# A third seven-product step in the gate and up projections of a two-layer decoder trunk

## The chip, the cores and the metric

The kernel runs on one core of a Trainium2 chip. The metric is the device time of one execution in microseconds (us); lower is better. All arithmetic is in float32: every weight matrix is split into a high part and a low part, and every product is made as three matmuls (high by high, high by low, low by high).

## The reference

```python
def swiglu(h, w_gate, w_up, w_down):
    return (jax.nn.silu(h @ w_gate) * (h @ w_up)) @ w_down

def reference(x, ...):
    for i in range(DEPTH):                      # DEPTH = 2
        h = rms_norm(x, norm_mix[i])
        mix = gla_mixer(h, ...) if i % 2 == 0 else fox_mixer(h, ...)
        x = x + mix
        h = rms_norm(x, norm_ffn[i])
        x = x + swiglu(h, ffn_w_gate[i], ffn_w_up[i], ffn_w_down[i])
    return x
```

The sequence has 256 rows, the model dimension is 2048 and the hidden dimension of the feed-forward part is 5632. The change touches `h @ w_gate` and `h @ w_up` alone.

## The kernel before

**Chunks.** Weights stream from memory in chunks of 256 x 512 floats (512 KB). SyncE loads a chunk into one of four slots of `raw`; ScalarE rounds it into `w_hi` (a copy, L791); VectorE subtracts to get `w_lo` (L1279); TensorE then uses it. Slots are reused in a ring of four: ScalarE may round chunk n only when TensorE has used chunk n-4 (semaphore `chunk_used`), TensorE may start chunk n when `lo_done` has counted it. Each engine runs its instructions in the order in which they are written.

**A gate/up tile.** The hidden dimension is cut in 11 tiles of 512 columns (FT = 11). A tile takes 16 chunks: eight of gate (t = 0) and eight of up (t = 1), chunk j holding rows 256 j to 256 j + 255 of the weight. TensorE gathers gate in `acc[:, 0]` and up in `acc[:, 1]`. A chunk taken plainly ("one") is four products of 128 x 128 by 128 x 512, so twelve matmuls. In tiles 1 to 9 of each layer some pairs of chunks (gate j and up j) are instead taken together in a "seven" step: a 2 x 2 block product (two row blocks of x against two column tiles) with seven products in place of eight, so 21 matmuls in place of 24. VectorE makes four differences of weight blocks for it (`g_raw`: L1429, L1432, L1435), ScalarE rounds them (`g_hi`, L870), VectorE makes their low parts (`g_lo`, L1444); of the second chunk of the pair only the lower half is split (L865, L1439). Four of the products go to banks of their own (`seven_acc`), and are added to gate and up at the end of the tile. The sums of x blocks that the seven products need (`xs_hi`, `xs_lo`) are made once per layer, during tile 0 (`x_sums`, L1398 to L1405, then L883 and L1412).

**Order.** `ORDER_GU` is the order of the 16 chunks of tiles 1 to 9, and all four engines walk it. Before, it is: gate 2 to 5; step 0; gate 6 and 7; step 1; up 2 to 7. The steps thus stand at positions 4, 5 and 8, 9 of the tile (positions count from 0).

**Work that hangs on positions.** On VectorE, at position 2 `hidden_joined` finishes the tile before: it adds `acc[:, 1]` to the sums (L1610) and multiplies by the activated gate (L1616, into `stage`, signal `staged`). At position 3 `squares_h` transposes `stage` (L1349), after which GpSimd issues sixteen small DMAs (L2028). At position 14 the first product is read out by ScalarE (L877) and added (L1452); at position 15 the other sums follow (L1457, L1459, L1461), gate is joined (L1464), and the transposed tile is split (L909, L1357). In tiles 1 and 2, `sums` (L1366 to L1369) follows there as well. Tile 1's position 2 has the plain `hidden` (L1584) for tile 0. `g_raw`, `g_lo` and the product sums `g_sum` lie in the same memory.

The ScalarE job `silu_joined` (L975) stands at position 1 and waits for `gate_joined`.

Of the kernel before, what the change touches and what calls it, by code (L numbers as in the profile page):

```python
# [30 lines left out]
F32 = mybir.dt.float32  # L31
F32R = mybir.dt.float32r
# [5 lines left out]
P = 128  # L38
# [38 lines left out]
def build(nc, x, norm_mix, norm_ffn, gla_w_in, gla_w_g2, gla_b_g2, gla_o_gain, gla_w_o,  # L77
# [38 lines left out]
    def down_order(steps, first, gaps):  # L116
# [3 lines left out]
        for j, gap in enumerate(gaps + (len(rest),)):  # L120
# [4 lines left out]
    ORDER = [[down_order(SEVEN, 6, (4, 4, 4))] * 2,  # L125
             [down_order(6, 8, (3, 3, 2, 2, 2)), down_order(8, 5, (2,) * 7)]]
    GU0, GU1 = 1, FT - 1
    PAIRS = 2
    GU = PAIRS * (GU1 - GU0)
    ORDER_GU = [("one", 0, j) for j in range(2, 6)] + [("seven", 0, 0), ("seven", 1, 0), ("one", 0, 6), ("one", 0, 7),  # L130
                                                       ("seven", 0, 1), ("seven", 1, 1)] \
        + [("one", 1, j) for j in range(2, CH)]

    def down_step(layer, pp, j):
        return layer * (GU + DT // 2 * SEVEN) + GU + pp * STEPS[layer][0] + j
# [21 lines left out]
    with ctx:  # L157
        def sb(name, shape, dt=F32):
            return ctx.enter_context(nc.sbuf_tensor(name, shape, dt))
# [33 lines left out]
        hscale = sb("head_scale", [P, TB * 4])  # L193
        gqk = sb("fox_gains", [P, 1])
        psc = sb("psc", [P, 3, TB * 4])
        narrow = sb("narrow", [R, S])
        diag = sb("diag", [P, TB, P])
        ohr = sb("o_rstd", [P, GH, TB])
# [75 lines left out]
        xs_hi, xs_lo = (at(f"x_sum_{i}", [P, PAIRS, 4, P], (32 + 44 * (i == "lo")) * K, F32R) for i in ("hi", "lo"))  # L274
        xs_raw = at("x_sum_raw", [P, PAIRS, 4, P], 76 * K)
# [125 lines left out]
        def _(pe):  # L401
# [82 lines left out]
            def gate_up(layer, c_up, i):  # L484

                c = gate_chunk(c_up, i)
                step = gate_step(layer, i)
                block0, block1 = slice(0, P), slice(P, S)
                upper, lower = slice(0, N), slice(N, 2 * N)
                for n, (kind, t, j) in enumerate(ORDER_GU):  # L490
                    a = (c.base + n) % SLOTS
                    if kind == "seven" and t == 0:
                        b, first, last = a + 1, j == 0, j == PAIRS - 1
                        k = KC_CHUNK * j
                        wait(pe, lo_done, c + (n + 2))
                        if isinstance(i, int) and first:
                            pe.wait_ge(x_sum_lo, layer + 1)
                        three(seven_acc[0], xt_hi[:, k, block0], xt_lo[:, k, block0], w_hi[:, a, upper],
                              w_lo[:, a, upper], first, last)
                        three(acc[:, 0, 0, :], xt_hi[:, k + 1, block0], xt_lo[:, k + 1, block0], w_hi[:, a, lower],  # L500
                              w_lo[:, a, lower], False, last).then_inc(chunk_used, 1)
                        three(acc[:, 1, 0, :], xs_hi[:, j, 3, :], xs_lo[:, j, 3, :], w_hi[:, b, lower],
                              w_lo[:, b, lower], first, False).then_inc(chunk_used, 1)
                        wait(pe, diff_lo, (step + (j + 1)) * 2 + (-1))
                        three(seven_acc[1], xs_hi[:, j, 0, :], xs_lo[:, j, 0, :], g_hi[:, 0, :], g_lo[:, 0, :], first, last)
                        three(seven_acc[3], xs_hi[:, j, 2, :], xs_lo[:, j, 2, :], g_hi[:, 1, :], g_lo[:, 1, :], first, last)
                        wait(pe, diff_lo, (step + (j + 1)) * 2)
                        three(seven_acc[2], xs_hi[:, j, 1, :], xs_lo[:, j, 1, :], g_hi[:, 2, :], g_lo[:, 2, :], first, last)
# [268 lines left out]
        def _(ac):  # L777
# [102 lines left out]
            def x_sums_hi(layer):  # L880

                ac.wait_ge(x_sum_raw, layer + 1)
                nc.scalar.activation(xs_hi[:, :, :, :], xs_raw[:, :, :, :], ACT.Copy).then_inc(x_sum_hi, 1)  # L883

            def squares(n, norm, t):

# [380 lines left out]
        def _(ve):  # L1267
# [126 lines left out]

            def x_sums(layer):

                both = slice(0, PAIRS * KC_CHUNK)
                link(nc.vector.tensor_tensor(hraw[:, both, :], xt_hi[:, both, :].bitcast(F32),  # L1398
                                             xt_lo[:, both, :].bitcast(F32), ALU.add))
                src = hraw[:, both, :].rearrange("p (j r) (b t) -> p j r b t", r=KC_CHUNK, t=P)  # L1400
                a11, a12, a21, a22 = (src[:, :, r, b, :] for b in range(TB) for r in range(KC_CHUNK))
                nc.vector.tensor_tensor(xs_raw[:, :, 2, :], a11, a21, ALU.subtract)
                link(nc.vector.tensor_tensor(xs_raw[:, :, 0, :], a21, a22, ALU.add))
                link(nc.vector.tensor_tensor(xs_raw[:, :, 1, :], xs_raw[:, :, 0, :], a11, ALU.subtract))
                nc.vector.tensor_tensor(xs_raw[:, :, 3, :], a12, xs_raw[:, :, 1, :],  # L1405
                                        ALU.subtract).then_inc(x_sum_raw, 1)

            def x_sums_low(layer):

                ve.wait_ge(x_sum_raw, layer + 1)  # L1410
                ve.wait_ge(x_sum_hi, layer + 1)
                nc.vector.tensor_tensor(xs_lo[:, :, :, :], xs_raw[:, :, :, :], xs_hi[:, :, :, :].bitcast(F32),  # L1412
                                        ALU.subtract).then_inc(x_sum_lo, 1)

            def gate_up(layer, c_up, i, hidden, turn, swap):
# [4 lines left out]
                for n, (kind, t, j) in enumerate(ORDER_GU):  # L1420
# [16 lines left out]
                    if (kind, t) == ("seven", 1):  # L1437
# [3 lines left out]
                        for half in range(2):  # L1441
# [1 line left out]
                            wait(ve, diff_hi, (step + (j + 1)) * 2 + (half - 1))  # L1443
                            nc.vector.tensor_tensor(g_lo[:, pair, :], g_raw[:, pair, :], g_hi[:, pair, :].bitcast(F32),  # L1444
                                                    ALU.subtract).then_inc(diff_lo, 1)
                    if n == 2:
                        hidden()
                    if n == 3:
                        swap()
                    if n == 14:  # L1450
                        wait(ve, p1_gate, gate_count(layer, i) + 1)
# [2 lines left out]
                    if n == 15:  # L1454
                        wait(ve, moved, gate_tile(layer, i) * 256)
                        wait(ve, gate_sums, sums + 1)
                        nc.vector.tensor_tensor(g_sum[:, 1, :], seven_acc[3], g_sum[:, 2, :],  # L1457
                                                ALU.add).then_inc(gate_sums, 1)
                        nc.vector.tensor_tensor(g_sum[:, 2, :], seven_acc[1], g_sum[:, 2, :], ALU.add)  # L1459
                        wait(ve, gate_sums, sums + 2)  # L1460
                        nc.vector.tensor_tensor(g_sum[:, 3, :], seven_acc[1], g_sum[:, 1, :],  # L1461
                                                ALU.add).then_inc(gate_sums, 1)
                        wait(ve, chunk_used, c + 10)
                        nc.vector.tensor_tensor(act[:, :, :], acc[:, 0, :, :], g_sum[:, 0:2, :],  # L1464
                                                ALU.add).then_inc(gate_joined, 1)
                    if n == 15:
# [93 lines left out]
            def out_and_ffn(c_o, g_o, c_up, g_up, c_down, g_down, m, norm, first, first_turn, saved):  # L1560
# [44 lines left out]
                def hidden_joined(i):  # L1605
# [1 line left out]
                    end = gate_chunk(c_up, i)  # L1607
                    wait(ve, chunk_used, end)
                    wait(ve, gate_sums, gate_count(layer, i, 3))
                    nc.vector.tensor_tensor(g_sum[:, 2:4, :], acc[:, 1, :, :], g_sum[:, 2:4, :],  # L1610
                                            ALU.add).then_inc(up_joined, 1)
                    wait(ve, gate_done, (Lin(i) if isinstance(i, int) else Lin(0, 1, i)) + layer * FT)
                    wait(ve, turned, (Lin(i) if isinstance(i, int) else Lin(0, 1, i)) + (g_up - 1))
                    wait(ve, up_joined, gate_count(layer, i))
                    for b in range(TB):
                        last = nc.vector.scalar_tensor_tensor(  # L1616
                            out=stage[:, b, :], in0=g_sum[:, 2 + b, :], scalar=rstd[:, norm, b:b + 1],
                            in1=act[:, b, :], op0=ALU.mult, op1=ALU.mult)
                    last.then_inc(staged, 1)

# [546 lines left out]
```

## Time and profile before

| | |
|---|---|
| median of 3 runs | 2277.46 us (2277.4 to 2277.67) |
| the profiled execution: its time, its span | 2278.0 us, 2275.7 us |
| TensorE matmul busy | 2267.3 us (100% of the span), 10242 matmuls |
| VectorE busy | 1737.7 us (76%) |
| ScalarE busy | 1211.2 us (53%) |
| GpSimd busy | 341.9 us (15%) |
| share of the 16 DMA engines, weights' queue | 61.9% |

The span is the time from the first to the last instruction of the profiled execution; the 2.3 us between it and the time of that execution lie outside of what the engines do. Busy matmul time counts the union of overlapping matmuls: a matmul is shown as 389 ns long, while the next one starts much sooner.

### The profile page before, as it was taken

How to read it: one execution, taken by the hardware profiler on the slowest of the kernel's cores; microseconds unless marked ns; L12 is line 12 of the kernel's file. 1: busy time of each engine (PE TensorE's matmuls, PEld its weight loads, DVE VectorE, ACT ScalarE, POOL GpSimd, SP SyncE). 2: the span in 40 equal slices, each digit the busy share in tenths (PEclk: the TensorE clock that was granted, in tenths of full speed). 3: DMA queues.
4: the chain of work that ended last, by engine and by line, in shares of the span. 5: the costliest groups of instructions: out<-in, count | busy, mean ns of one | idle time of the engine just before them, and what ended most of it. 6: DMA issues, size and time to landing. Idle time of an engine off the chain costs nothing.

```text
span 2275.7 us, 28590 instructions
## 1 busy us (share of the span) xinstructions
PE 2267.3 (100%) x10242; PEld 1878.1 (83%) x10242; DVE 1737.7 (76%) x2049; ACT 1211.2 (53%) x1563; POOL 341.9 (15%) x558
## 2 busy tenths in 40 slices
PE   9999999999999999999999999999999999999999
PEld 7888878888888888888888888888888888888887
DVE  6888558688888877887577855568788888868787
ACT  5545554555555554454566656445555555545454
POOL 2036210111211211000223200001112112111000
PEclk9999999999999999999999999999999999999999
DMA  7655545666666666565758876655666666666664
GB/s 220 185 176 158 174 158 185 199 215 215 199 225 204 209 220 214 189 202 195 193 170 208 213 181 166 155 174 191 219 196 221 214 202 212 221 203 205 218 205 158
DMA packets 241211, 447.53 MB, mean 197 GB/s; under 512 B 23236, under 2 KB 25384, under 8 KB 241112
## 3 DMA queue, kind: packets, MB, share of 16 engines
q1 hardware_dynamic: 224416, 430.49, 61.9%
q0 software_dynamic: 12304, 15.24, 2.0%
q10 hardware_dynamic: 4392, 0.50, 0.2%
q8 instruction: 58, 0.95, 0.2%
q14 instruction: 41, 0.34, 0.0%
HBM read 432.52 MB, written 2.11 MB: 191 GB/s over the span
## 4 chain that ended last, share of the span: by engine, by line
PE 98%; DVE 1%; ACT 1%; DMA 0%; issue 0%; ACTq 0%; SPq 0%
PE acc L451 16%; PE acc L452 16%; PE acc L453 16%; PE acc L442 14%; PE acc L444 14%; PE acc L443 14%; PE wk L453 1%; PE wk L452 1%; PE tp L453 1%; PE tp L452 1%; PE wk L451 1%; PE tp L451 1%; PE wk L671 1%; DVE w_lo L1279 0%; PE tp L409 0%; PE wk L728 0%
## 5 line engine op out<-in xcount | busy, mean ns | idle before, releaser
L1279 DVE TENSOR_TENSOR w_lo<-raw,w_hi 128x1024 fp32r<-128x1024 f32 x758 | 933.0, 1249 | 394.7 <-ACT w_hi L791 389.9
L791 ACT ACTIVATE w_hi<-raw 128x1024 fp32r<-128x1024 f32 x758 | 796.7, 1060 | 701.5 <-PE acc L453 339.7
L442 PE MATMUL acc<-w_hi,xt_hi 128*128 128x512 f32 x1152 | 454.7, 395 | 2.2 <-DVE w_lo L1279 2.1
L444 PE MATMUL acc<-w_hi,xt_lo 128*128 128x512 f32 x1152 | 448.8, 390 | 0.0
L443 PE MATMUL acc<-w_lo,xt_hi 128*128 128x512 f32 x1152 | 448.4, 389 | 0.0
L451 PE MATMUL acc<-w_hi,xt_hi 128*128 128x512 f32 x900 | 350.1, 389 | 0.0
L452 PE MATMUL acc<-w_lo,xt_hi 128*128 128x512 f32 x900 | 350.1, 389 | 0.0
L453 PE MATMUL acc<-w_hi,xt_lo 128*128 128x512 f32 x900 | 350.1, 389 | 0.0
L2028 POOL DMA_DIRECT2D ht_raw<-act x352 | 173.0, 499 | 775.8 <-DVE act L1349 746.0
L442 PEld LDWEIGHTS acc<-w_hi,xt_hi 128*128 128x128 f32 x1152 | 216.3, 188 | 50.7 <-issue 3.3
L444 PEld LDWEIGHTS acc<-w_hi,xt_lo 128*128 128x128 f32 x1152 | 216.2, 188 | 45.5
L443 PEld LDWEIGHTS acc<-w_lo,xt_hi 128*128 128x128 f32 x1152 | 216.4, 188 | 44.7 <-issue 1.0
L451 PE MATMUL acc<-w_hi,ht_hi 128*128 128x512 f32 x550 | 213.9, 389 | 0.0
L452 PE MATMUL acc<-w_lo,ht_hi 128*128 128x512 f32 x550 | 213.9, 389 | 0.0
L453 PE MATMUL acc<-w_hi,ht_lo 128*128 128x512 f32 x550 | 213.9, 389 | 0.0
L453 PEld LDWEIGHTS acc<-w_hi,xt_lo 128*128 128x128 f32 x900 | 168.9, 188 | 35.3
L452 PEld LDWEIGHTS acc<-w_lo,xt_hi 128*128 128x128 f32 x900 | 168.9, 188 | 35.1
L451 PEld LDWEIGHTS acc<-w_hi,xt_hi 128*128 128x128 f32 x900 | 168.9, 188 | 34.9
L451 PEld LDWEIGHTS acc<-w_hi,ht_hi 128*128 128x128 f32 x550 | 103.2, 188 | 21.6
L452 PEld LDWEIGHTS acc<-w_lo,ht_hi 128*128 128x128 f32 x550 | 103.2, 188 | 21.4
L453 PEld LDWEIGHTS acc<-w_hi,ht_lo 128*128 128x128 f32 x550 | 103.2, 188 | 21.3
L870 ACT ACTIVATE gate_diff_hi<-gate_diff_raw 128x1024 fp32r<-128x1024 f32 x72 | 76.6, 1063 | 59.4 <-DVE gate_diff_raw L1429 45.1
(322 smaller groups left out, 2666.8 us busy)
## 6 DMA issues: line engine op xcount, KB each, us to landing
raw<-in_ffn_w_gate_dram SPq DMA_DIRECT2D x176, 512.0 KB, 3.9
raw<-in_ffn_w_up_dram SPq DMA_DIRECT2D x176, 512.0 KB, 4.6
raw<-in_ffn_w_down_dram SPq DMA_DIRECT2D x176, 512.0 KB, 4.4
raw<-in_fox_w_in_dram SPq DMA_DIRECT2D x128, 512.0 KB, 5.5
raw<-in_gla_w_in_dram SPq DMA_DIRECT2D x96, 512.0 KB, 4.5
raw<-in_gla_w_o_dram SPq DMA_DIRECT2D x32, 512.0 KB, 4.2
raw<-in_fox_w_o_dram SPq DMA_DIRECT2D x32, 512.0 KB, 4.0
ht_raw<-act POOLq DMA_DIRECT2D x352, 32.0 KB, 3.3
```

What stands on the lines that cost most here:

```text
L442: pe.matmul(o, xh, wh, start=(k == 0), stop=False)
L443: pe.matmul(o, xh, wl, start=False, stop=False)
L444: last = pe.matmul(o, xl, wh, start=False, stop=(k == chunks * KC_CHUNK - 1))
L451: pe.matmul(o, xh, wh, start=start, stop=False)
L452: pe.matmul(o, xh, wl, start=False, stop=False)
L453: return pe.matmul(o, xl, wh, start=False, stop=stop)
L671: last = pe.matmul(wk[:, b, h * P:(h + 1) * P], ks, qs, start=(kf == 0), stop=(kf == FPH - 1))
L791: nc.scalar.activation(w_hi[:, slot, :], raw[:, slot, :], ACT.Copy).then_inc(hi_done, 1)
L870: nc.scalar.activation(g_hi[:, two, :], g_raw[:, two, :], ACT.Copy).then_inc(diff_hi, 1)
L1279: nc.vector.tensor_tensor(w_lo[:, slot, :], raw[:, slot, :], w_hi[:, slot, :].bitcast(F32), ALU.subtract).then_inc(lo_done, 1)
L2028: po.dma_start(hraw[Q * j:Q * j + Q, i, :], ht_sq[Q * i:Q * i + Q, j, :]).then_inc(moved, 16)
```

## The change

`PAIRS` goes from 2 to 3, so each of tiles 1 to 9 takes three pairs of chunks in seven-product steps. The new order is: gate 3; step 0; gate 4 and 5; step 1; gate 6 and 7; step 2; up 3 to 7. The steps stand at positions 1, 2, then 5, 6, then 9, 10. `hidden_joined` moves from position 2 to 3 and `squares_h` from 3 to 4. TensorE gets a new wait on `staged` in the first step, ahead of the product that overwrites `acc[:, 1, 0]`; VectorE waits for `gate_joined` before the first differences. Two of the product sums go to `stage` instead of `g_sum`, and the gated product is made in place there. The sums of x for the third pair get memory of their own.

```diff
-    PAIRS = 2
+    PAIRS = 3
-    ORDER_GU = [("one", 0, j) for j in range(2, 6)] + [("seven", 0, 0), ("seven", 1, 0), ("one", 0, 6), ("one", 0, 7),
-                                                       ("seven", 0, 1), ("seven", 1, 1)] \
-        + [("one", 1, j) for j in range(2, CH)]
+    ORDER_GU = [("one", 0, 3)]
+    for j in range(PAIRS):
+        ORDER_GU += [("seven", 0, j), ("seven", 1, j)] + [("one", 0, 4 + 2 * j + m) for m in range(2) if j + 1 < PAIRS]
+    ORDER_GU += [("one", 1, j) for j in range(PAIRS, CH)]
@@ sums of x for the third pair
+        xs2_hi = at("x_sum2_hi", [P, 1, 4, P], 92 * K, F32R)
+        xs2_lo, xs2_raw = over("x_sum2_lo", [P, 1, 4, P], x_sum_at, F32R), over("x_sum2_raw", [P, 1, 4, P], x_sum_at)
@@ TensorE, gate_up, in a seven step
                         three(acc[:, 0, 0, :], xt_hi[:, k + 1, block0], xt_lo[:, k + 1, block0], w_hi[:, a, lower],
                               w_lo[:, a, lower], False, last).then_inc(chunk_used, 1)
-                        three(acc[:, 1, 0, :], xs_hi[:, j, 3, :], xs_lo[:, j, 3, :], w_hi[:, b, lower],
+                        if first:
+                            wait(pe, staged, Lin(G[f"ffn{layer}"] + i) if isinstance(i, int) else Lin(G[f"ffn{layer}"], 1, i))
+                        three(acc[:, 1, 0, :], sum_h[:, 3, :], sum_l[:, 3, :], w_hi[:, b, lower],
                               w_lo[:, b, lower], first, False).then_inc(chunk_used, 1)
@@ ScalarE, x_sums_hi
-                nc.scalar.activation(xs_hi[:, :, :, :], xs_raw[:, :, :, :], ACT.Copy).then_inc(x_sum_hi, 1)
+                nc.scalar.activation(xs_hi[:, :, :, :], xs_raw[:, :, :, :], ACT.Copy)
+                nc.scalar.activation(xs2_hi[:, :, :, :], xs2_raw[:, :, :, :], ACT.Copy).then_inc(x_sum_hi, 1)
@@ VectorE, x_sums
-                both = slice(0, PAIRS * KC_CHUNK)
-                link(nc.vector.tensor_tensor(hraw[:, both, :], xt_hi[:, both, :].bitcast(F32),
-                                             xt_lo[:, both, :].bitcast(F32), ALU.add))
+                link(nc.vector.tensor_tensor(hraw[:, :, :], xt_hi[:, 0:4, :].bitcast(F32), xt_lo[:, 0:4, :].bitcast(F32),
+                                             ALU.add))
+                link(x_pairs(hraw[:, :, :], xs_raw))
+                rest = slice(4, PAIRS * KC_CHUNK)
+                link(nc.vector.tensor_tensor(hraw[:, 0:KC_CHUNK, :], xt_hi[:, rest, :].bitcast(F32),
+                                             xt_lo[:, rest, :].bitcast(F32), ALU.add))
+                x_pairs(hraw[:, 0:KC_CHUNK, :], xs2_raw).then_inc(x_sum_raw, 1)
+
+            def x_pairs(x, dst):
+
+                src = x.rearrange("p (j r) (b t) -> p j r b t", r=KC_CHUNK, t=P)
                 a11, a12, a21, a22 = (src[:, :, r, b, :] for b in range(TB) for r in range(KC_CHUNK))
+                nc.vector.tensor_tensor(dst[:, :, 2, :], a11, a21, ALU.subtract)
+                link(nc.vector.tensor_tensor(dst[:, :, 0, :], a21, a22, ALU.add))
+                link(nc.vector.tensor_tensor(dst[:, :, 1, :], dst[:, :, 0, :], a11, ALU.subtract))
+                return nc.vector.tensor_tensor(dst[:, :, 3, :], a12, dst[:, :, 1, :], ALU.subtract)
@@ VectorE, x_sums_low: a second subtraction of 128 x 512 for xs2_lo
@@ VectorE, gate_up
                         wait(ve, diff_used, step + j)
+                        if j == 0:
+                            wait(ve, gate_joined, gate_count(layer, i))
...
-                    if n == 2:
+                    if n == 3:
                         hidden()
-                    if n == 3:
+                    if n == 4:
                         swap()
...
-                        nc.vector.tensor_tensor(g_sum[:, 2, :], seven_acc[1], g_sum[:, 2, :], ALU.add)
+                        wait(ve, turned, gate_tile(0, i) + G[f"ffn{layer}"])
+                        nc.vector.tensor_tensor(stage[:, 0, :], seven_acc[1], g_sum[:, 2, :], ALU.add)
                         wait(ve, gate_sums, sums + 2)
-                        nc.vector.tensor_tensor(g_sum[:, 3, :], seven_acc[1], g_sum[:, 1, :],
+                        nc.vector.tensor_tensor(stage[:, 1, :], seven_acc[1], g_sum[:, 1, :],
                                                 ALU.add).then_inc(gate_sums, 1)
-                        wait(ve, chunk_used, c + 10)
+                        wait(ve, chunk_used, c + 11)
@@ VectorE, hidden_joined
-                    nc.vector.tensor_tensor(g_sum[:, 2:4, :], acc[:, 1, :, :], g_sum[:, 2:4, :],
+                    nc.vector.tensor_tensor(stage[:, :, :], acc[:, 1, :, :], stage[:, :, :],
                                             ALU.add).then_inc(up_joined, 1)
...
-                            out=stage[:, b, :], in0=g_sum[:, 2 + b, :], scalar=rstd[:, norm, b:b + 1],
+                            out=stage[:, b, :], in0=stage[:, b, :], scalar=rstd[:, norm, b:b + 1],
```

## Rows read from the trace of the kernel before

**Rows 1.** The page: busy time of the engines, and the granted clock in 40 slices.

```profile
PE 2267.3 (100%) x10242; PEld 1878.1 (83%) x10242; DVE 1737.7 (76%) x2049; ACT 1211.2 (53%) x1563; POOL 341.9 (15%) x558
...
PEclk9999999999999999999999999999999999999999
```

**Rows 2.** The page: the chain that ended last, by engine.

```profile
PE 98%; DVE 1%; ACT 1%; DMA 0%; issue 0%; ACTq 0%; SPq 0%
```

**Rows 3.** Busy time by stretch: one whole gate/up tile of layer 0.

```profile
603.50:645.70 42.20, 42.20 (x188) 34.95 (x187) 35.75 (x38) 22.87 (x25) 7.84 (x16) 1.00 0.67 211
```

**Rows 4.** Timeline of PE: start, length, engine, line, names, count; 614.71 starts a tile.

```profile
600.65 0.39 PE L452 MATMUL acc<-w_lo,xt_hi 128*128 128x512 f32 x1
...
614.71 0.39 PE L451 MATMUL acc<-w_hi,xt_hi 128*128 128x512 f32 x1
...
622.41 0.39 PE L452 MATMUL acc<-w_lo,xt_hi 128*128 128x512 f32 x1
```

**Rows 5.** Timeline of DVE around the same start of a tile; idle before in brackets.

```profile
605.12 1.23 DVE L1279 TENSOR_TENSOR w_lo<-raw,w_hi 128x1024 fp32r<-128x1024 f32 x1 [0.89 <-ACT w_hi L791]
...
610.32 2.35 DVE L1279 TENSOR_TENSOR w_lo<-raw,w_hi 128x1024 fp32r<-128x1024 f32 x2
...
615.00 1.23 DVE L1610 TENSOR_TENSOR gate_product_sums<-acc,gate_product_sums 128x1024 f32<-128x1024 f32 x1 [0.50 <-PE acc L453]
616.26 1.42 DVE L1616 SCALAR_TENSOR_TENSOR stage<-gate_product_sums,rstd,act 128x512 f32<-128x512 f32 x2
617.60 1.22 DVE L1279 TENSOR_TENSOR w_lo<-raw,w_hi 128x1024 fp32r<-128x1024 f32 x1
618.73 1.30 DVE L1349 STREAM_TRANSPOSE act<-stage 128x512 f32<-128x512 f32 x2
...
621.05 1.22 DVE L1429 TENSOR_TENSOR gate_diff_raw<-raw 128x1024 f32<-128x1024 f32 x1
...
623.64 0.69 DVE L1439 TENSOR_TENSOR w_lo<-raw,w_hi 128x512 fp32r<-128x512 f32 x1
...
626.51 2.36 DVE L1279 TENSOR_TENSOR w_lo<-raw,w_hi 128x1024 fp32r<-128x1024 f32 x2
```

**Rows 6.** Timeline of ACT in the same tile: second half of a step, next rounding.

```profile
623.76 1.06 ACT L870 ACTIVATE gate_diff_hi<-gate_diff_raw 128x1024 fp32r<-128x1024 f32 x1 [0.39 <-DVE gate_diff_raw L1435]
...
628.42 1.06 ACT L791 ACTIVATE w_hi<-raw 128x1024 fp32r<-128x1024 f32 x1 [1.57 <-DMA raw<-in_ffn_w_gate_dram]
```

**Rows 7.** Timeline of DVE at the end of tile 1, layer 0: `sums`.

```profile
483.90 0.42 DVE L1366 TENSOR_TENSOR sum_raw<-ht_raw 128x256 f32<-128x256 f32 x1
...
485.49 3.49 DVE L1279 TENSOR_TENSOR w_lo<-raw,w_hi 128x1024 fp32r<-128x1024 f32 x3
```

**Rows 8.** Timelines of DVE, ACT, PE, end of tile 0 (layer 0); 446.07 starts tile 1.

```profile
434.96 1.22 DVE L1398 TENSOR_TENSOR ht_raw<-xt_hi,xt_lo 128x1024 f32<-128x1024 f32 x1
...
437.47 0.42 DVE L1405 TENSOR_TENSOR x_sum_raw<-ht_raw,x_sum_raw 128x256 f32<-128x256 f32 x1
...
441.11 1.22 DVE L1412 TENSOR_TENSOR x_sum_lo<-x_sum_raw,x_sum_hi 128x1024 fp32r<-128x1024 f32 x1
...
446.27 1.41 DVE L1584 SCALAR_TENSOR_TENSOR stage<-acc,rstd,act 128x512 f32<-128x512 f32 x2 [0.34 <-PE acc L444]
...
438.89 3.06 ACT L791 ACTIVATE w_hi<-raw 128x1024 fp32r<-128x1024 f32 x3
...
446.07 0.39 PE L451 MATMUL acc<-w_hi,xt_hi 128*128 128x512 f32 x1
```

**Rows 9.** Timelines of DVE and PE: a wait of TensorE near the start of the kernel.

```profile
21.63 1.23 DVE L1279 TENSOR_TENSOR w_lo<-raw,w_hi 128x1024 fp32r<-128x1024 f32 x1
...
23.00 0.47 PE L442 MATMUL acc<-w_hi,xt_hi 128*128 128x512 f32 x1 [0.70 <-DVE w_lo L1279]
23.31 0.40 PE L443 MATMUL acc<-w_lo,xt_hi 128*128 128x512 f32 x1
```

**Rows 10.** Groups by line and shape: a subtraction or sum of 128 x 128 on DVE.

```profile
L1924 DVE TENSOR_TENSOR fox_p<-fox_p,masks 128x128 f32<-128x128 f32 x16 | 4.7, 292 | 0.5
```

More of the change, by code:

```diff
@@ L127, in build @@
     GU0, GU1 = 1, FT - 1
-    PAIRS = 2
+    PAIRS = 3
     GU = PAIRS * (GU1 - GU0)
-    ORDER_GU = [("one", 0, j) for j in range(2, 6)] + [("seven", 0, 0), ("seven", 1, 0), ("one", 0, 6), ("one", 0, 7),
-                                                       ("seven", 0, 1), ("seven", 1, 1)] \
-        + [("one", 1, j) for j in range(2, CH)]
+    ORDER_GU = [("one", 0, 3)]
+    for j in range(PAIRS):
+        ORDER_GU += [("seven", 0, j), ("seven", 1, j)] + [("one", 0, 4 + 2 * j + m) for m in range(2) if j + 1 < PAIRS]
+    ORDER_GU += [("one", 1, j) for j in range(PAIRS, CH)]
+    assert len(ORDER_GU) == 2 * CH
     def down_step(layer, pp, j):
@@ L195, in build @@
         psc = sb("psc", [P, 3, TB * 4])
+        x_sum_at = nc.sbuf_base
         narrow = sb("narrow", [R, S])
@@ L273, in build @@
         g_raw, g_sum = at("gate_diff_raw", [P, 4, N], 80 * K), at("gate_product_sums", [P, 4, N], 80 * K)
-        xs_hi, xs_lo = (at(f"x_sum_{i}", [P, PAIRS, 4, P], (32 + 44 * (i == "lo")) * K, F32R) for i in ("hi", "lo"))
-        xs_raw = at("x_sum_raw", [P, PAIRS, 4, P], 76 * K)
+        xs_hi, xs_lo = (at(f"x_sum_{i}", [P, 2, 4, P], (32 + 44 * (i == "lo")) * K, F32R) for i in ("hi", "lo"))
+        xs_raw = at("x_sum_raw", [P, 2, 4, P], 76 * K)
+        xs2_hi = at("x_sum2_hi", [P, 1, 4, P], 92 * K, F32R)
+        assert base + room[0] <= nc.sbuf_usable_end
+        xs2_lo, xs2_raw = over("x_sum2_lo", [P, 1, 4, P], x_sum_at, F32R), over("x_sum2_raw", [P, 1, 4, P], x_sum_at)
+        XS = [(xs_hi[:, 0], xs_lo[:, 0]), (xs_hi[:, 1], xs_lo[:, 1]), (xs2_hi[:, 0], xs2_lo[:, 0])]
         d_hi = over("diff_hi", [P, 4, N], xt_at + xt_half, F32R)
@@ L493, in gate_up @@
                         b, first, last = a + 1, j == 0, j == PAIRS - 1
+                        sum_h, sum_l = XS[j]
                         k = KC_CHUNK * j
@@ L501, in gate_up @@
                               w_lo[:, a, lower], False, last).then_inc(chunk_used, 1)
-                        three(acc[:, 1, 0, :], xs_hi[:, j, 3, :], xs_lo[:, j, 3, :], w_hi[:, b, lower],
+                        if first:
+                            wait(pe, staged, Lin(G[f"ffn{layer}"] + i) if isinstance(i, int) else Lin(G[f"ffn{layer}"], 1, i))
+                        three(acc[:, 1, 0, :], sum_h[:, 3, :], sum_l[:, 3, :], w_hi[:, b, lower],
                               w_lo[:, b, lower], first, False).then_inc(chunk_used, 1)
                         wait(pe, diff_lo, (step + (j + 1)) * 2 + (-1))
-                        three(seven_acc[1], xs_hi[:, j, 0, :], xs_lo[:, j, 0, :], g_hi[:, 0, :], g_lo[:, 0, :], first, last)
-                        three(seven_acc[3], xs_hi[:, j, 2, :], xs_lo[:, j, 2, :], g_hi[:, 1, :], g_lo[:, 1, :], first, last)
+                        three(seven_acc[1], sum_h[:, 0, :], sum_l[:, 0, :], g_hi[:, 0, :], g_lo[:, 0, :], first, last)
+                        three(seven_acc[3], sum_h[:, 2, :], sum_l[:, 2, :], g_hi[:, 1, :], g_lo[:, 1, :], first, last)
                         wait(pe, diff_lo, (step + (j + 1)) * 2)
-                        three(seven_acc[2], xs_hi[:, j, 1, :], xs_lo[:, j, 1, :], g_hi[:, 2, :], g_lo[:, 2, :], first, last)
+                        three(seven_acc[2], sum_h[:, 1, :], sum_l[:, 1, :], g_hi[:, 2, :], g_lo[:, 2, :], first, last)
                         three(acc[:, 0, 1, :], xt_hi[:, k + 1, block1], xt_lo[:, k + 1, block1], g_hi[:, 3, :],
@@ L1395, in x_sums @@
             def x_sums(layer):
-                both = slice(0, PAIRS * KC_CHUNK)
-                link(nc.vector.tensor_tensor(hraw[:, both, :], xt_hi[:, both, :].bitcast(F32),
-                                             xt_lo[:, both, :].bitcast(F32), ALU.add))
-                src = hraw[:, both, :].rearrange("p (j r) (b t) -> p j r b t", r=KC_CHUNK, t=P)
-                a11, a12, a21, a22 = (src[:, :, r, b, :] for b in range(TB) for r in range(KC_CHUNK))
[L1402 to L1406, printed above, removed]
+                link(nc.vector.tensor_tensor(hraw[:, :, :], xt_hi[:, 0:4, :].bitcast(F32), xt_lo[:, 0:4, :].bitcast(F32),
[7 more added lines that the diff above has]
+                src = x.rearrange("p (j r) (b t) -> p j r b t", r=KC_CHUNK, t=P)
+                a11, a12, a21, a22 = (src[:, :, r, b, :] for b in range(TB) for r in range(KC_CHUNK))
+                nc.vector.tensor_tensor(dst[:, :, 2, :], a11, a21, ALU.subtract)
+                link(nc.vector.tensor_tensor(dst[:, :, 0, :], a21, a22, ALU.add))
+                link(nc.vector.tensor_tensor(dst[:, :, 1, :], dst[:, :, 0, :], a11, ALU.subtract))
+                return nc.vector.tensor_tensor(dst[:, :, 3, :], a12, dst[:, :, 1, :], ALU.subtract)
             def x_sums_low(layer):
@@ L1411, in x_sums_low @@
                 ve.wait_ge(x_sum_hi, layer + 1)
-                nc.vector.tensor_tensor(xs_lo[:, :, :, :], xs_raw[:, :, :, :], xs_hi[:, :, :, :].bitcast(F32),
+                nc.vector.tensor_tensor(xs_lo[:, :, :, :], xs_raw[:, :, :, :], xs_hi[:, :, :, :].bitcast(F32), ALU.subtract)
+                nc.vector.tensor_tensor(xs2_lo[:, :, :, :], xs2_raw[:, :, :, :], xs2_hi[:, :, :, :].bitcast(F32),
                                         ALU.subtract).then_inc(x_sum_lo, 1)
```

## The prediction, as put on record before the result was known

> **What bounds the kernel now.** The page comes first: TensorE's matmuls cover the whole span and the granted clock is in its top tenth in every slice, the 2.4 GHz level [rows 1]. The chain that ended last is 98% TensorE [rows 2]. So time is the number of matmuls times their spacing, plus every wait of TensorE. The spacing is read from start to start, not from the 0.39 us that a matmul is shown to last: the first and the last of these rows are 96 matmuls apart, 21.76 us, so 0.2267 us each [rows 4]. A gate/up tile of 186 matmuls then takes 42.16 us, and the stretch of one tile agrees, with TensorE busy throughout [rows 3]. TensorE has no slack to give, and each matmul less is worth 0.2267 us as long as nobody makes it wait.
>
> Who could? In that tile VectorE is busy 35.75 of 42.2 us, ScalarE 22.87 [rows 3]. VectorE is the next one, so the question is how much work it gets and, more, where. VectorE's idle time there stands before splits of weight chunks, waiting for ScalarE, which waits for TensorE to free one of four slots [rows 5]. The 6.4 us of slack can thus not be saved up: VectorE runs at most three chunks ahead.
>
> **What is removed.** Each third step makes 21 matmuls of 24. That is 3 x 9 tiles x 2 layers = 54 matmuls, 54 x 0.2267 = 12.2 us, all on the path: a gain if nothing else happens.
>
> **What is added to VectorE and ScalarE.** A step, from the first difference to the next plain split, takes VectorE 626.51 - 621.05 = 5.46 us, where the one plain split it replaces takes 618.73 - 617.60 = 1.13 [rows 5]. So 4.33 us more per tile: 35.8 + 4.3 = 40.1 of a tile that would be 183 x 0.2267 = 41.5 us long. It fits as a sum, with 1.4 us to spare. ScalarE gets two roundings of 1.06 us [rows 6] and saves about half of one, some 1.7 us on 22.9, which hides.
>
> **Where it falls.** I count from the first matmul of a tile, 614.71 before [rows 4]. The last split of the tile before starts at 605.12, so at -9.59, held back by a slot and not by VectorE's own backlog (0.89 idle) [rows 5]. That hold stays, because the tile's last five chunks stay plain. Between it and the first split of the new tile (610.32, at -4.39) VectorE works without a gap on the product sums, the joined gate and the turned tile [rows 5]. The same instructions stand there after the change; that two of them write to `stage` I cost at nothing, since size and source stay (bounds: 0 to 0.1 us a tile).
>
> From there the order is new. Splits 0 and 1: 2 x 1.13, to -2.13. Step 0: 5.46, to 3.33. Split 3: 1.13, to 4.46. Only now comes `hidden_joined`, whose two parts take from 615.00 to 616.26 + 1.42, or 2.68 us [rows 5]: `staged` at 7.14. ScalarE keeps up: its last rounding for a step starts at 623.76, 2.71 after the step's first difference [rows 6], so it ends at -2.13 + 2.71 + 1.06 = 1.64, and the rounding of chunk 3, about 1 us, is done by 2.7.
>
> TensorE takes chunk 0 (12 matmuls) and the first six of step 0, and then stands at its new wait on `staged`, at 18 x 0.2267 = 4.08. What is queued behind it are the other 15 matmuls of the step and the whole rest of the tile; ScalarE's roundings wait for those through the slots. From the end of a VectorE split to TensorE's first matmul after a real wait it takes 23.00 - (21.63 + 1.23) = 0.14 us, and the second matmul comes 0.31 after the first in place of 0.23, 0.08 more [rows 9]. So TensorE resumes at 7.28: **a wait of 3.20, with the restart 3.28 us, in each ordinary tile**, against 0.68 us saved there. The rest of step 0 is not late: the half split it needs ends at -2.13 + (623.64 - 621.05) + 0.69 = 1.15 [rows 5], asked at 2.72; the low differences end by about 3.4, asked at 4.76 and 6.12. Even with nothing else to do VectorE could not sign before 0.3 + 2.68, the old place [rows 5].
>
> Steps 1 and 2 I cost at nothing. Their cover is the two plain chunks between steps, 5.4 us, as long as VectorE's 5.46 of a step starts at once when TensorE leaves the step before. The low parts of differences are then ready some 2 us before they are asked. Without this cover a late step would cost its lateness. The third load pair is requested when the half split of the step before is done and lands some 4 us later (ScalarE waits for such a load until 628.42, 4.1 us after that split's end at 624.33) [rows 5, 6]; in the new order that is 6 us or more before TensorE needs the split, so DMA stays hidden. Bounds: 0 to 1 us a tile.
>
> **Tiles 2 and 3** come after the tiles in which VectorE also makes `sums`: 485.49 - 483.90 = 1.59 us more between joined gate and first split [rows 7]. That hides today and no longer will: 3.28 + 1.59 = 4.87 us each.
>
> **Tile 1** has the longer `x_sums` ahead of it [rows 8]. Today they end at 437.47 + 0.42 = 437.89 and ScalarE rounds the last chunk of tile 0 from 438.89. The third pair adds a sum of 128 x 512 (0.69 us as the split of that size [rows 5]) and four of 128 x 128 (0.29 each [rows 10]), about 1.95 us in all, and to ScalarE about 0.55. So that rounding starts at 441.4, its split ends at 443.7, and TensorE, asking at 446.07 - 2.72 = 443.35, waits 0.5. The low parts (1.13 + 0.6) come next, then splits 0 and 1: TensorE waits another 0.2 for the first and starts the tile at 446.74; step 0 starts at 447.65. Its half split ends at 450.93, with 0.14 at 451.07, asked at 449.46: 1.6. `staged` comes at 447.65 + 5.46 + 1.13 + 1.41 (the plain form, L1584 [rows 8]) = 455.65, with 0.14 at 455.79, asked at 452.43: 3.35. Four waits and restarts: 0.5 + 0.2 + 1.6 + 3.35 + 0.3 = 5.95. Bounds 4.5 to 7.
>
> **The sum.** A layer: 5.95 + 2 x 4.87 + 6 x 3.28 = 35.4; two layers 70.7. Less 12.2: +58.5. Against the profiled execution's own 2278.0 us that is 2336.5; the median of the runs lies 0.5 us lower, so **2336**. The terms' bounds (steady wait 3.0 to 3.6, tile 1, restart) give 2329 to 2344 for this case by itself.
>
> **Rivals.**
>
> *TensorE's clock falls.* The new waits are of 3.3 to 4.9 us, one a tile. The gaps that the trace shows are near the start and short (0.70 us in the row), and the clock holds [rows 1, 9]; so no row shows what a long one does. Half the clock for as long again as the wait would lose half of that time: for the four longest waits 4 x 4.9 / 2 = 10 us, 2346; for all eighteen (66 us of waits on `staged`) 33 us, 2369. Against it: each gap is followed by 41 us of dense matmuls, and most are only just over 3 us. Chance 14%. The Trainium skill, page "TensorE: Matmul & The Clock Gate", section "HAM oscillation — how this bites in real kernels", states this mechanism: waits that are long enough bring the array back to half its clock, over and over in one kernel. By that rule some of the longer waits here would be followed by matmuls at 1.2 GHz; no run here shows it.
>
> *Steps 1 or 2 become late too.* VectorE has 1.4 us to spare in a tile, and loads are asked for in pairs. If a load lands 1 to 2 us later than [rows 6] show, step 2 starts late. At 1 us a tile, 18 us more: 2354. For it speaks the tight sum, against it the 3.3 us by which the wait itself lengthens the tile, which is room for VectorE. Chance 8%.
>
> *No wait, only the gain.* This ends on the other side. VectorE would have to sign `staged` by 3.94 after the start of the tile, 3.2 earlier than I work out; it decides in its favour if step 0's work is mostly done before the tile starts. VectorE does have 6.4 us idle in a tile [rows 3], so a different gating of the last splits could allow it. Then 2278.0 - 12.2 = 2265.8, some 2265. With waits of just 0.68 us a tile, nothing would change. Against it: the splits 15, 0 and 1 and the differences stand in one queue, and 605.12 is set by TensorE's progress [rows 5]. Chance 4% for this, 3% for about no change.
>
> *Shorter waits.* If part of the queue is faster than read (step 0 overlapping more), 1 to 2 us a tile: 2290 to 2320. Chance 6%.
>
> **How the numbers follow.** The forecast has 65%, the rivals 14, 8, 4, 3 and 6. About 0.2% is what a measurement of this kernel can tell from no change, 4.6 us. Slower by more than that: 65 + 14 + 8 + 6, less a little, is 92%; within 3%, faster 5%. The range reaches from the upper part of shorter waits over the case itself (2329 to 2344) to late steps and a clock that falls a few times: 2320 to 2357.
>
> **What would show it.** In the profile after: 10188 matmuls; TensorE's waits led by one on VectorE's L1616-form (`stage`), some 16 times at 3.3 us and for four of them near 4.9, plus two for the plain form in tile 1; VectorE going from the joined gate to the in-place product without a gap; a tile of 44.8 us against 42.2. The prediction is wrong if that wait is missing or under 2 us, if TensorE's other waits sum to more than 10 us, or if the granted clock leaves its top level in the gate/up stretches.

## The result, and the profile after

The changed kernel takes 2373.51 us (median of 4 runs, 2367.37 to 2374.78) against 2277.57 us (median of 4): 4.15% slower, ratio 1.0415 with a 95% interval of 1.0403 to 1.0428. The forecast was 2336 us with a range of 2320 to 2357. The direction and the place were right; the size was 61% of what came, and the time lies outside the range.

The page after: busy time, the granted clock, the chain (they answer to [rows 1, 2]).

```profile
PE 2301.6 (97%) x10188; PEld 1893.6 (80%) x10188; DVE 1818.3 (77%) x2151; ACT 1242.9 (52%) x1601; POOL 342.2 (14%) x558
...
PEclk9999999999999999999999999999999998999999
...
PE 84%; DVE 10%; issue 3%; ACT 1%; DVEq 0%; DMA 0%; ACTq 0%; SPq 0%
```

There are 54 matmuls less, and yet TensorE is busy 34.3 us longer: the matmuls themselves must have become slower. The clock digits hide it, except for one slice with an 8, because a tenth is coarse. The list of TensorE's waits names who kept it:

```profile
PE acc L458 <- DVE stage L1637: 54.1, 16, 4.4
PE acc L458 <- DVE stage L1605: 6.1, 2, 3.1
PE tp L458 <- DVE w_lo L1459: 2.6, 2, 1.3
PE acc L449 <- DVE w_lo L1290: 2.1, 5, 1.0
```

That is the list the prediction asked for: 16 waits on the in-place product, 2 on the plain form in tile 1, 2 on the half split of tile 1. Only the last line's 2.1 us were there before. VectorE around the start of a tile after (the tile begins at 637.16, 18 matmuls before the wait; it answers to [rows 5]):

```profile
627.58 1.23 DVE L1290 TENSOR_TENSOR w_lo<-raw,w_hi 128x1024 fp32r<-128x1024 f32 x1 [2.49 <-ACT w_hi L801]
...
632.77 2.35 DVE L1290 TENSOR_TENSOR w_lo<-raw,w_hi 128x1024 fp32r<-128x1024 f32 x2
635.05 1.22 DVE L1449 TENSOR_TENSOR gate_diff_raw<-raw 128x1024 f32<-128x1024 f32 x1
...
638.24 2.35 DVE L1464 TENSOR_TENSOR gate_diff_lo<-gate_diff_raw,gate_diff_hi 128x1024 fp32r<-128x1024 f32 x2
640.51 1.22 DVE L1290 TENSOR_TENSOR w_lo<-raw,w_hi 128x1024 fp32r<-128x1024 f32 x1
641.64 1.22 DVE L1631 TENSOR_TENSOR stage<-acc,stage 128x1024 f32<-128x1024 f32 x1
642.97 1.41 DVE L1637 SCALAR_TENSOR_TENSOR stage<-stage,rstd,act 128x512 f32<-128x512 f32 x2
```

No bracket after the first row: from the last split of the old tile to the signature VectorE never stands still. And TensorE in the same tile (it answers to [rows 4]; the last matmul before the wait, then those after it):

```profile
641.01 0.39 PE L460 MATMUL acc<-w_hi,xt_lo 128*128 128x512 f32 x1
644.43 0.79 PE L458 MATMUL acc<-w_hi,x_sum_hi 128*128 128x512 f32 x1 [3.03 <-DVE stage L1637]
645.03 0.63 PE L459 MATMUL acc<-w_lo,x_sum_hi 128*128 128x512 f32 x1
645.45 0.63 PE L460 MATMUL acc<-w_hi,x_sum_lo 128*128 128x512 f32 x1
...
649.72 0.63 PE L458 MATMUL acc<-gate_diff_hi,xt_hi 128*128 128x512 f32 x1
650.15 0.46 PE L459 MATMUL acc<-gate_diff_lo,xt_hi 128*128 128x512 f32 x1
650.44 0.39 PE L460 MATMUL acc<-gate_diff_hi,xt_lo 128*128 128x512 f32 x1
650.67 0.40 PE L458 MATMUL acc<-w_hi,xt_hi 128*128 128x512 f32 x1
```

The wait is 644.43 - 641.01 - 0.23 = 3.19 us, where 3.20 was forecast. But the next matmuls stand 0.43 us apart, not 0.23, until 650.15. The windows say why (us, then busy time of PE, PEld, DVE, ACT, POOL, then the granted clock, DMA share, GB/s):

```profile
641.24:644.43 3.19, 0.16 (x1) 0.00 (x0) 3.09 (x5) 1.06 (x1) 0.00 (x0) 0.85 0.92 299
644.43:650.28 5.85, 5.84 (x14) 4.59 (x15) 3.41 (x4) 0.63 (x1) 3.24 (x7) 0.50 0.48 143
650.28:688.80 38.52, 38.52 (x171) 31.66 (x169) 33.36 (x35) 22.85 (x24) 4.61 (x10) 1.00 0.59 184
```

The clock fell to 0.50, 1.2 GHz, near the end of the wait and stayed there for 14 matmuls; then it was back at 2.4 GHz for the rest of the tile. It does not always fall within the wait. One tile earlier it was full throughout the same wait and fell about 1.1 us after TensorE had resumed:

```profile
594.76:597.96 3.20, 0.17 (x2) 0.01 (x1) 3.10 (x5) 1.06 (x1) 0.00 (x0) 1.00 0.94 312
597.96:602.50 4.54, 4.54 (x13) 3.62 (x14) 3.40 (x4) 0.63 (x1) 1.96 (x5) 0.62 0.52 155
```

The records of the granted clock show a low stretch, of 3.4 or 6.8 us, in or just behind each of the 18 waits on `staged`, at the longer and the shorter ones alike, 88.7 us in all; the kernel before has none but a last one as the program ends.

### The profile page after: what moved, and what is told of

It reads as the page before. It is cut to its first block, busy times and chain, and to the rows that moved or that the text cites. A ratio compares the mean times of both kernels' runs of the same rounds, so it can differ in the third digit from the quotient of the medians.

```text
span 2373.1 us, 28767 instructions
## 1 busy us (share of the span) xinstructions
PE 2301.6 (97%) x10188; PEld 1893.6 (80%) x10188; DVE 1818.3 (77%) x2151; ACT 1242.9 (52%) x1601; POOL 342.2 (14%) x558
## 4 chain that ended last, share of the span: by engine, by line
PE 84%; DVE 10%; issue 3%; ACT 1%; DVEq 0%; DMA 0%; ACTq 0%; SPq 0%
PE acc L449 13%; PE acc L451 13%; PE acc L450 13%; PE acc L458 11%; PE acc L459 11%; PE acc L460 11%; DVE w_lo L1290 3%; PE wk L458 2%; PE wk L459 2%; PE wk L460 2%; PE tp L460 1%; PE tp L459 1%; PE tp L458 1%; ACT w_hi L801 1%; DVE gate_diff_lo L1464 1%
## 5 line engine op out<-in xcount | busy, mean ns | idle before, releaser
L1290 DVE TENSOR_TENSOR w_lo<-raw,w_hi 128x1024 fp32r<-128x1024 f32 x740 | 911.1, 1249 | 360.1 <-ACT w_hi L801 355.9
L801 ACT ACTIVATE w_hi<-raw 128x1024 fp32r<-128x1024 f32 x740 | 777.4, 1060 | 613.6 <-PE acc L460 261.4
L449 PE MATMUL acc<-w_hi,xt_hi 128*128 128x512 f32 x1152 | 455.0, 395 | 2.4 <-DVE w_lo L1290 2.1
L451 PE MATMUL acc<-w_hi,xt_lo 128*128 128x512 f32 x1152 | 448.7, 390 | 0.0
L450 PE MATMUL acc<-w_lo,xt_hi 128*128 128x512 f32 x1152 | 448.5, 389 | 0.0
L458 PE MATMUL acc<-w_hi,xt_hi 128*128 128x512 f32 x774 | 301.4, 389 | 0.0
L459 PE MATMUL acc<-w_lo,xt_hi 128*128 128x512 f32 x774 | 301.2, 389 | 0.0
L460 PE MATMUL acc<-w_hi,xt_lo 128*128 128x512 f32 x774 | 301.1, 389 | 0.0
L449 PEld LDWEIGHTS acc<-w_hi,xt_hi 128*128 128x128 f32 x1152 | 216.3, 188 | 51.5 <-DVE w_lo L1290 4.3
L451 PEld LDWEIGHTS acc<-w_hi,xt_lo 128*128 128x128 f32 x1152 | 216.3, 188 | 45.8
L450 PEld LDWEIGHTS acc<-w_lo,xt_hi 128*128 128x128 f32 x1152 | 216.4, 188 | 44.3 <-issue 1.0
L880 ACT ACTIVATE gate_diff_hi<-gate_diff_raw 128x1024 fp32r<-128x1024 f32 x108 | 114.9, 1063 | 174.5 <-DVE gate_diff_raw L1449 153.5
L458 PEld LDWEIGHTS acc<-w_hi,xt_hi 128*128 128x128 f32 x774 | 145.4, 188 | 31.1 <-DVE w_lo L1290 0.5
L460 PEld LDWEIGHTS acc<-w_hi,xt_lo 128*128 128x128 f32 x774 | 145.3, 188 | 30.3
L459 PEld LDWEIGHTS acc<-w_lo,xt_hi 128*128 128x128 f32 x774 | 145.3, 188 | 30.2
L1464 DVE TENSOR_TENSOR gate_diff_lo<-gate_diff_raw,gate_diff_hi 128x1024 fp32r<-128x1024 f32 x108 | 127.1, 1219 | 0.0
```

What stands on the lines that cost most here:

```text
L449: pe.matmul(o, xh, wh, start=(k == 0), stop=False)
L450: pe.matmul(o, xh, wl, start=False, stop=False)
L451: last = pe.matmul(o, xl, wh, start=False, stop=(k == chunks * KC_CHUNK - 1))
L458: pe.matmul(o, xh, wh, start=start, stop=False)
L459: pe.matmul(o, xh, wl, start=False, stop=False)
L460: return pe.matmul(o, xl, wh, start=False, stop=stop)
```

## The experiments

Theory A: the waits cost what was forecast, and the rest, about 37 us, is the array at 1.2 GHz after each. Rival B: the rest is steps 1 and 2, late because VectorE is nearly full or loads land late.

**Filling the wait.** TensorE gets extra matmuls in front of the wait, whose result nobody reads.

```diff
                         if first:
+                            for _ in range(14):
+                                pe.matmul(seven_acc[3], xt_hi[:, k, block0], w_hi[:, b, lower], start=True, stop=True)
                             wait(pe, staged, ...)
```

> The changed kernel, with 14 extra matmuls of 512 columns into a bank that the step writes anew afterwards, put just ahead of TensorE's wait on `staged` in each of the 18 tiles; they take the place of most of the wait and add no result. Theory A (the waits are as long as forecast, and the rest of the loss is the array at 1.2 GHz after each of them): the wait of about 3.2 us shrinks to about 0.1 us in ordinary tiles and about 1.7 in tiles 2 and 3, the granted clock stays at its top level, and the time is 2332 to 2340 us, some 37 less than the changed kernel, though TensorE gets 252 matmuls more to do. Rival B (the rest of the loss is steps 1 and 2, late because VectorE is nearly full, or loads that land late): filling the wait changes nothing of that, 2368 to 2376 us.

2337.04 us, one run, granted clock 1.000. So with 252 matmuls more it is 36.5 us faster. Its list of waits:

```profile
PE acc L458 <- DVE stage L1639: 5.0, 4, 1.3
PE tp L458 <- DVE w_lo L1461: 2.6, 2, 1.3
```

In the twelve ordinary tiles no wait is listed any more, but its time is still spent, now on the extra matmuls (an ordinary tile takes 44.86 us, forecast 44.8). Nothing of what B names was touched, and B expected 2368 us or more: B is out. The price of the clock is 36.5 us, the distance to the changed kernel's median; against its single runs it is 30.3 to 37.7 us. Half as many matmuls:

> As the one with 14 extra matmuls, with 7 of them: the rest of the wait is about 1.6 us in ordinary tiles and 3.2 in tiles 2 and 3. Theory A: the clock falls in fewer tiles or in none but the four long ones, 2334 to 2350 us. If a rest of 1.6 us is enough to bring the clock down in every tile, the time stays near 2365 to 2372. Rival B: 2368 to 2376 whatever the filling.

2342.36 us, one run, clock 0.998.

```profile
PE acc L458 <- DVE stage L1639: 28.7, 16, 2.8
PE acc L458 <- DVE stage L1607: 3.0, 2, 1.5
```

After the fourteen rests of about 1.4 us (twelve of the first line, two of the second) the clock holds; of the four of about 2.8 us it falls in three (the records of the granted clock, 10.2 us low in all). One of these (start of tile 2, layer 0):

```profile
502.80 0.79 PE L458 MATMUL acc<-w_hi,x_sum_hi 128*128 128x512 f32 x1 [2.85 <-DVE stage L1639]
503.39 0.63 PE L459 MATMUL acc<-w_lo,x_sum_hi 128*128 128x512 f32 x1
```

Three falls for some 5 us more: about 1.7 us each.

**The early place without the third step.** Two steps as before, sums of x for two pairs, step 0 at positions 1 and 2.

```diff
-    PAIRS = 3
+    PAIRS = 2
+    ORDER_GU = [("one", 0, 2), ("seven", 0, 0), ("seven", 1, 0), ("one", 0, 3), ..., ("one", 0, 7),
+                ("seven", 0, 1), ("seven", 1, 1)] + [("one", 1, j) for j in range(PAIRS, CH)]
```

> The changed kernel without the third step: two steps as before, the first at positions 1 and 2 (the early place), the second at positions 8 and 9, sums of x for two pairs. It has the 10242 matmuls of the kernel before and VectorE's load of before. Theory A (the early place of step 0 costs, not the number of steps): waits on `staged` of 3.2 us in ordinary tiles and 4.8 in tiles 2 and 3 remain, with the clock falling after each, 2374 to 2390 us, slower than the changed kernel. Rival B (the third step's work fills VectorE, and that costs): 2278 to 2300 us.

2365.72 us, one run, 88 us slower than before with the same 10242 matmuls and VectorE's old load. Its waits:

```profile
PE acc L456 <- DVE stage L1629: 54.1, 16, 4.4
PE acc L456 <- DVE stage L1597: 4.5, 2, 2.3
```

The 54.1 us are those of the changed kernel to the tenth. So the place of the first step makes the wait, not the number of steps. The forecast of 2374 to 2390 was 8 us or more too high, again through the clock: with tiles of another length it fell at 14 of the 18 waits and was low for 51.2 us in the two layers' tiles, not for 88.7; over the first layer's tiles it was 0.97 of full where the changed kernel has 0.95. Equal waits do not bring equal falls.

**The product that waits, moved last.** The product that overwrites the up accumulator goes, with its wait, behind the other six.

```diff
-                        if first:
-                            wait(pe, staged, ...)
-                        three(acc[:, 1, 0, :], sum_h[:, 3, :], ...).then_inc(chunk_used, 1)
                         ...
                         three(acc[:, 0, 1, :], ...).then_inc(diff_used, 1)
+                        if first:
+                            wait(pe, staged, ...)
+                        three(acc[:, 1, 0, :], sum_h[:, 3, :], ...).then_inc(chunk_used, 1)
```

> The changed kernel, with the one product that overwrites the up accumulator, and the wait on `staged` ahead of it, moved behind the other six products of step 0 (of every step, in fact). It is asked for at 30 matmuls after the start of the tile, 6.80 us, instead of 18, 4.08 us, and `staged` still comes at about 7.3. Theory A: waits of 0.5 us in ordinary tiles, about 2.1 in tiles 2 and 3, about 3 in tile 1, in sum 22 us; the clock holds; less 12.2 us of removed matmuls that is 2284 to 2292 us. Rival B: 37 us remain on top of that, 2320 to 2328.

2299.17 us, ratio to before 1.0093 (1.0077 to 1.0110), clock 1.000: 74 us less than the changed kernel for one reordering. It is still 7 us above the forecast's top. A tile has two short waits where one was forecast:

```profile
629.85 0.50 PE L458 MATMUL acc<-w_hi,x_sum_hi 128*128 128x512 f32 x1 [0.31 <-DVE stage L1637]
...
636.50 0.50 PE L458 MATMUL tp<-w_hi,xt_hi 128*128 128x512 f32 x1 [0.21 <-DVE w_lo L1459]
```

The second is the half split of step 1, which VectorE now reaches too late: the long wait had given it room. And each costs more than it shows. An ordinary tile takes 42.75 us, 1.27 above 41.48, for 0.52 us of idle shown: about 0.37 us more per wait. Of this, 0.16 comes from the counting, since idle starts at a matmul's shown end, 0.16 after the next could start, and 0.11 from the restart, since the second matmul comes 0.34 after the first in place of 0.23. The rest was not traced.

**The join moved forward.** On VectorE, `hidden_joined` goes between the half split and the low parts of step 0.

```diff
                     if (kind, t) == ("seven", 1):
                         ... half split of the weights ...
+                        if j == 0:
+                            hidden()
                         for half in range(2):
                             ... low parts ...
-                    if n == 3:
-                        hidden()
```

> The changed kernel, with VectorE's joining of the tile before (`hidden_joined`, 2.68 us) moved from position 3 into step 0, between the half split and the low parts of the differences. Then `staged` comes at about 3.9 us after the start of the tile, asked for at 4.08: no wait there. The low differences come about 2.7 us later than in the changed kernel, 0.3 us after they are asked, and step 1's half split comes 0.3 to 0.6 late, as in the kernel with the product moved last. The clock holds. 0.3 + 0.4 us and two restarts of 0.2 to 0.4 a tile, 1.5 more in tiles 2 and 3, 3 in tile 1: 2288 to 2302 us. Rival: the wait on `staged` is due to something else in VectorE's queue, then 2320 or more.

2297.64 us, ratio 1.0088 (1.0073 to 1.0104), inside the range. The wait on `stage` is left in tiles 2 and 3 alone, 4.0 us in all; 10.7 us wait on half splits, 20 times: step 1 is late in the ordinary tiles.

**Everything spread.** On top of that, the transposing goes to position 6, the split of the turned tile to 13, the sums of x forward.

```diff
-                    if n == 4:
+                    if n == 6:
                         swap()
@@ ScalarE: turn() at 13 in place of 14; VectorE:
-                    if n == 15:
+                    if n == 13:
                         turn()
@@ tile 0, up half
-                tile(Lin(c_up), CH, mid=lambda: x_sums(norm // 2), ...)
+                tile(Lin(c_up), CH, late=lambda: x_sums(norm // 2), ...)
```

> As the one with the join first, and three more things moved to where VectorE sits idle: the transposing of the joined tile from position 4 to 6, behind step 1; the splitting of the turned tile (with `sums` in tiles 1 and 2) from position 15 (ScalarE: 14) to 13; the sums of x from position 6 to 3 in the second half of tile 0. All three steps and the 10188 matmuls stay. By the bookkeeping of VectorE's queue nothing is late in ordinary tiles, and some 0.6 us in tiles 2 and 3 at most: 2264 to 2270 us, faster than both kernels by the 12 us of the removed matmuls less a little. Rival (VectorE is too full for a third step wherever the pieces stand, 40.1 of 41.5 us a tile): waits of 0.5 us or more a tile remain, 2275 us or more.

2289.10 us, ratio 1.0053 (1.0039 to 1.0067): 19 us above its range. The time is one that the rival allowed (2275 us or more), but the trace gives another reason than a full VectorE. From start to start, nine of the eighteen tiles take 41.5 to 41.7 us, the other nine 42.0 to 44.9. GpSimd in a tile of 41.5 us that starts at 657.69, then ScalarE and VectorE in the same tile, and TensorE in the next one, which starts at 699.23 and takes 44.9:

```profile
673.56 1.96 POOL L2050 DMA_DIRECT2D ht_raw<-act  x4 [33.46 <-DVE act L1361]
679.48 5.87 POOL L2050 DMA_DIRECT2D ht_raw<-act  x12 [3.96 <-issue]
...
689.63 1.06 ACT L921 ACTIVATE ht_hi<-ht_raw 128x1024 f32 x1 [4.66 <-DMA ht_raw<-act]
690.59 1.04 ACT L801 ACTIVATE w_hi<-raw 128x1024 fp32r<-128x1024 f32 x1
...
690.93 1.23 DVE L1369 TENSOR_TENSOR ht_lo<-ht_raw,ht_hi 128x1024 f32 x1 [4.70 <-ACT ht_hi L921]
...
703.46 0.50 PE L458 MATMUL tp<-w_hi,xt_hi 128*128 128x512 f32 x1 [1.31 <-DVE w_lo L1460]
706.11 0.50 PE L458 MATMUL acc<-w_hi,x_sum_hi 128*128 128x512 f32 x1 [0.99 <-DVE stage L1638]
```

GpSimd stands still for 4 us between its fourth and fifth DMA. The moved tile lands 16 us after the transposing, ScalarE waits for it at position 13, and the roundings queued behind it are late; VectorE waits for them, and so comes late to the next tile. The same holds for all three such pauses in each layer's tiles 1 to 9: the six tiles behind them take 43.7 to 44.9 us, some 18 us too many in sum. The pauses are in the kernel before as well (2.0 to 4.5 us in the same three tiles of layer 0), where the tile has time to land.

**Spread, with room for the landing.** Two kernels, both with the transposing between step 1's half split and its low parts, and ScalarE's `turn()` at 14. In the first VectorE splits the turned tile at position 14, behind the first sum; in the second at 15, behind the joined gate.

```diff
                         if j == 0:
                             hidden()
+                        if j == 1:
+                            swap()
...
                     if n == 14:
                         wait(ve, p1_gate, ...)
                         ... L1473, the first sum ...
+                        turn()
```

> The spread kernel before it lost some 4 us in every second tile: GpSimd paused for 4 us between two of its sixteen small DMAs, the moved tile landed some 16 us after the transposing, and ScalarE, in order, stood before the split of the turned tile at position 13 and held the last roundings. Here the transposing stands within step 1, between its half split and its low parts (2.3 us earlier), and the split of the turned tile at position 14, on ScalarE behind the read-out of the first product, on VectorE behind the first sum. Theory: the landing at about 30 us of the tile no longer holds anything, ordinary tiles take 41.5 to 41.8 us in both kinds, tiles 2 and 3 about 2 us more: 2268 to 2276 us, faster than before. Rival: the low parts of step 1, now 1.2 us later, or the landing are late after all, 0.5 us or more a tile, 2277 to 2288.

> As the one with the transposing within step 1, but VectorE splits the turned tile where it always did, behind the joined gate. VectorE then reaches step 0 about 1.1 us later in each tile; `staged` still comes in time (about 3.8 us, asked at 4.08) and the first low parts are about 0.3 us late: 0.3 to 0.6 us a tile, and one more in tiles 2 and 3: 2272 to 2282 us. If the landing was what held the kernel with all spread, both of this pair are free of it.

The first takes 2266.49 us (2266.34 to 2267.02, 5 runs), ratio 0.9951 (0.9937 to 0.9965): 0.5% faster than the kernel before, by 11.1 of the 12.2 us that the removed matmuls promise, and 1.5 us below its own range, since tiles 2 and 3 do not wait either. All that TensorE still waits for lies in the first 142 us, far ahead of these tiles:

```profile
PE wk L620 <- POOL ident L2058: 1.6, 1, 1.6
PE tp L613 <- DMA xres<-in_x_dram: 1.3, 1, 1.3
PE acc L449 <- DVE w_lo L1291: 1.2, 2, 1.0
PE acc L449 <- ACT xt_hi L1055: 1.0, 1, 1.0
```

And VectorE, whose load in these tiles was the reason to doubt a third step, is nearly full:

```profile
440.00:814.00 374.00, 373.94 (x1648) 309.10 (x1647) 358.13 (x385) 217.74 (x232) 70.67 (x144) 1.00 0.66 215
```

358.1 of 374.0 us, 96%, with TensorE at full speed. So a VectorE as full as this does not by itself cost anything. The second kernel takes 2279.19 us, ratio 1.0006 (0.9997 to 1.0015), inside its range: no change against before. The two differ in one piece of VectorE's work of 1.1 us. In the first it stands ahead of the tile's last split, where VectorE would wait for ScalarE; in the second behind that split and the joined gate, where it delays the next tile's step 0. That is worth 12.7 us: an ordinary tile takes 41.9 us in place of 41.5, and tiles 2 and 3 take 43.6 and 43.5. Both kernels leave the landing more time than the one with everything spread; which of the moves that this took made the other 10 us was not tried one by one.

## Why the prediction was wrong

- **Matmuls saved, 12.2 us.** Right: 10188 matmuls, and the first of the last two kernels collects 11.1 us.
- **VectorE's queue.** Right to a tenth. From the last split of the old tile (627.58) to the end of the join (644.38) it takes 16.80 us, forecast -9.59 to 7.14, 16.73. `stage` in place of `g_sum` cost nothing.
- **The wait, 3.20 us in ordinary tiles.** Right: 3.19. In tiles 2 and 3 1.4 more shown (4.4 against 3.0), forecast 1.59. Tile 1: waits of 0.2, 1.3 and 3.1 us shown and a late start, forecast 0.5, 0.2, 1.6 and 3.35. The list shows 54.1 us for the sixteen waits and 7.4 us for all that wait on anything but `stage`, under the 10 that the prediction allowed.
- **Steps 1 and 2 at nothing.** Right here, because the wait itself made the room; wrong once the wait is gone (the product moved last, the join moved forward). They were costed at their cover, but the cover was partly the stall.
- **What failed: "Two layers 70.7", in which every matmul after a wait still counts 0.2267 us.** The sum took the spacing of [rows 4] for all 10188 matmuls. After each of the 18 waits some 7 to 14 ran at 0.43, because the granted clock was 0.50 there. The run with the waits filled is 2337.04 us, the forecast 2336; so practically the whole error is this term, 36.5 us. From the trace: half of the low time in which TensorE worked is 20 us in the first layer, worked out tile by tile (1.7, 1.5, 1.5, 1.7, 2.9, 3.0, 3.1, 3.1, 1.4), and the second layer repeats it. That makes 40 us, where the two profiled runs differ by 37.7; the gap of some 2 us stays open. The prediction's own sign of being wrong, a granted clock that leaves its top level in the gate/up stretches, came true.
- **The rival had it.** "TensorE's clock falls" gave 33 us and 2369 for all eighteen and was held at 14%, with the argument that most waits are only just over 3 us. No row of the kernel before bore on that, so the chance should have been nearer even and the range should have reached 2369; even then it would have ended 4.5 us below the measured time. That 33 us came so near to 36.5 is partly luck: the rival let the low clock last as long as the wait, while it lasted 3.4 us behind the waits of 4.4 us and 3.4 or 6.8 behind those of 3.2. The Trainium skill, page "TensorE: Matmul & The Clock Gate", section "HAM oscillation — how this bites in real kernels", tells of a kernel that waits for data in every tile of its loop and falls back to the lower clock in every one; the trace of the changed kernel agrees, 18 times of 18, with the clock at 0.50, and the kernel with two early steps, at 14 of 18, does so in part.

## What to carry to other kernels

A step that makes an accumulator's overwrite earlier needs the previous reader earlier too: write down when the reader signs, in the order of its engine's queue, before counting the saved matmuls. When a forecast contains TensorE waits of about 3 us or more, price the matmuls after them at the lower clock as well (here the clock fell at 18 of 18 such waits, at 14 of 18 and at three of four); if the wait cannot be removed, spare matmuls in it cost nothing and here gave back 36.5 us. And work added to a nearly full engine goes where that engine now idles, but not in front of something that waits for a many-part transfer.

## What the runs showed of the hardware

- The granted clock fell to 0.50 in waits of TensorE of 3.2 us and more or up to 1.2 us behind them, each time in the changed kernel; with 1.4 us of idle left it never fell (0 of 14), with 2.8 us in three of four. With the same waits and another tile length (the two early steps) it fell at 14 of 18 and was low for 51.2 us in place of 88.7. Why equal waits differ was not tried.
- The changed kernel's own runs spread over 7.4 us (2367.37 to 2374.78), those of the kernel before over 0.5 us; the mean granted clock differs with them (0.985 in the fastest run, 0.981 in the slowest).
- GpSimd, issuing sixteen small DMAs half a microsecond apart, pauses for 2 to 4.5 us in some tiles, and in the same place before and after: in layer 0 behind the tenth, the fourth and the fourteenth DMA of the same three tiles, and behind the eighth of the layer's last tile. What it does meanwhile was not found out.
